# Encoder kernel: first projection units as native FP32 products, a branch split one stage earlier, side units split at the front of their stage

## What is computed

```python
h = rmsnorm(x, norm_g[l])
proj = jnp.einsum('bsd,de->bse', h, w_in[l])          # 42 units, 16 columns ba, 24 gate units
o_a = windowed_gqa(...);  y_a = einsum(o_a * silu(a_z), w_bo_a[l])
o_b = diff_attention(...); y_b = einsum(o_b * silu(b_z), w_bo_b[l])
o_c = rmsnorm(o_fwd + o_bwd, c_norm_g[l])             # two gated delta rules
y_c = einsum(o_c * silu(c_z), w_bo_c[l])
merged = gates[0] * y_a + gates[1] * y_b + gates[2] * y_c
x = x + einsum(merged, w_out[l])
# after both layers: rmsnorm(x, final_g)
```

## Time and profile before

| | us |
|---|---|
| median of 3 runs | 2986.66 |
| lowest, highest | 2984.34, 2987.62 |
| profiled execution, its own time | 2982.72 |
| span in the trace of that execution | 2980.8 |
| PE busy in the span | 2722.8 |
| POOL busy in the span | 1375.6 |
| granted TensorE clock, mean | 0.965 of 2.4 GHz |

### The profile page before, as it was taken

How to read it: one execution, slowest core, us unless ns; L and a number is a source line. 1 busy time by engine, 2 the same in 40 slices (tenths; PEclk the granted TensorE clock), 3 DMA queues, 4 the chain that set the end, 5 groups by cost and what they waited for, 6 DMA issues and landing times. The chain is left out here.

```text
span 2980.8 us, 40155 instructions
## 1 busy us (share of the span) xinstructions
PE 2722.8 (91%) x15402; PEld 2219.3 (74%) x15402; DVE 1593.7 (53%) x1859; ACT 1130.2 (38%) x1866; POOL 1375.6 (46%) x1226
## 2 busy tenths in 40 slices
PE   6989998999889899899879999899998899998995
PEld 4868786777768788777667787777776777896784
DVE  5137646776467443375241565377754864234743
ACT  3024434666345314331111344266653543244111
POOL 4355335343478740265354543444434886304551
PEclk8999999999989999999989999999999999999997
DMA  5253224221344556654242531333213554567431
GB/s 185 71 156 99 79 71 136 85 93 64 124 156 159 170 165 161 227 172 125 68 135 86 148 107 64 112 102 99 86 58 120 193 171 159 164 165 258 129 112 72
DMA packets 394918, 380.51 MB, mean 128 GB/s; under 512 B 91104, under 2 KB 333408, under 8 KB 394720
## 3 DMA queue, kind: packets, MB, share of 16 engines
q1 hardware_dynamic: 355744, 295.87, 33.1%
q10 hardware_dynamic: 38976, 82.00, 7.4%
HBM read 247.70 MB, written 130.09 MB: 127 GB/s over the span
## 5 line engine op out<-in xcount | busy, mean ns | idle before, releaser
L266 PE MATMUL pair<-h_hi,w_hi 128*128 128x512 f32 x1792 | 741.9, 414 | 117.3 <-ACT ev L281 44.8
L246 POOL TENSOR_TENSOR w_hi<-w_stage,masks 128x256 fp32r<-128x256 f32 x432 | 403.6, 965 | 727.3 <-PE pair L266 655.8
L266 PE MATMUL pair<-h_lo,w_hi 128*128 128x512 f32 x1792 | 710.7, 397 | 0.0
L266 PE MATMUL pair<-h_hi,w_lo 128*128 128x512 f32 x1792 | 709.9, 396 | 0.0
L266 PEld LDWEIGHTS pair<-h_hi,w_hi 128*128 128x128 f32 x1792 | 344.1, 192 | 241.7 <-issue 100.8
L266 PEld LDWEIGHTS pair<-h_hi,w_lo 128*128 128x128 f32 x1792 | 343.6, 192 | 75.7
L266 PEld LDWEIGHTS pair<-h_lo,w_hi 128*128 128x128 f32 x1792 | 344.7, 192 | 70.7 <-issue 5.1
L251 POOL TENSOR_TENSOR w_lo<-w_stage,w_hi 128x256 fp32r<-128x256 f32 x432 | 354.5, 852 | 8.5
L281 ACT ACTIVATE ev<-pair 128x512 f32<-128x512 f32 x224 | 132.6, 593 | 492.0 <-PE pair L266 491.8
L217 PE MATMUL pair<-h_hi,w_hi 128*128 128x512 f32 x576 | 183.1, 399 | 41.7 <-DVE h_lo L593 23.9
L2291 POOL TENSOR_TENSOR w_hi<-w_stage,masks 128x512 fp32r<-128x512 f32 (+1 forms) x60 | 103.6, 1727 | 221.0 <-PE pair L217 191.0
(11 more groups left out here) (283 smaller groups left out, 4940.1 us busy)
## 6 DMA issues: line engine op xcount, KB each, us to landing
w_stage<-in_w_in SPq DMA_DIRECT2D x132, 512.0 KB, 4.1
proj<-ev ACTq DMA_DIRECT2D x132, 512.0 KB, 2.7
gate<-proj SPq DMA_DIRECT2D x48, 512.0 KB, 3.6
prep_x<-proj SPq DMA_DIRECT2D x24, 512.0 KB, 4.0
resid<-xT SPq DMA_DIRECT2D x16, 512.0 KB, 8.1
diff_vx<-proj SPq DMA_DIRECT2D x16, 512.0 KB, 3.2
prep_g<-gc_rows SPq DMA_DIRECT2D x16, 512.0 KB, 5.2
qd_t<-prep_eg SPq DMA_DIRECT2D x16, 512.0 KB, 2.6
```

The lines of the kernel that those rows point to most:

```text
L246: last = nc.gpsimd.tensor_tensor(w_hi[s][:, part], w_stage[s][:, part], bcast(ones, PIECE), ALU.mult)
L266: last = nc.tensor.matmul(bank(self.banks[half]), a[s][:, c, :], b[:, c, w], start=(c == 0 and n == 0), stop=(c == KC - 1 and n == 2))
```

## The change

Four things are changed together.

1. **proj.** The load of g and of the weights of units 0 and 1 moves to the end of the stage before (`load_first`, in load and in merge). Units 0 and 1 are no longer split: POOL multiplies their weights by g (`w_g`), PE multiplies them with the unnormalized `xT` in native FP32, and DVE multiplies the results by rstd. The sum of squares comes after chunk 0 of both units. The normalization runs in 16 half chunks through PSUM (`hf` in banks 4 and 5, `rstd_near` in pairs[3]); DVE makes all of `h_lo`. The ba product waits for all of it. POOL sets the next stage's semaphores later, within the stage.
2. **Side units.** win, diff and delta get the scheme of prep. The last split in diff was already absent; those of win (`split(17)`) and prep (`split(17)`) go, and `split(1)` stands at the front of POOL's list in win and diff, and after the memsets in delta. POOL's loop in proj keeps its range up to i = 5 for both slots.
3. **Branch 0** is loaded, rounded and subtracted at the end of delta, into the place of h_hi and h_lo, no longer at the start of merge.
4. **merge.** Heads 0, (1, 2), 3 are gated after steps 4, 5, 6 instead of 0, 1, 2, 3 after 4, 5, 6, 7. For i = OUT the second four chunks of the weights are split before the wait for the slot's last sum.

```diff
-        AHEAD["win"] = SIDE_AHEAD
+        AHEAD["win"] = SIDE_AHEAD_IN
-        AHEAD["diff"] = SIDE_AHEAD
+        AHEAD["diff"] = SIDE_AHEAD_IN
-        AHEAD["delta"] = SIDE_AHEAD
+        AHEAD["delta"] = SIDE_AHEAD_IN
-        AHEAD["merge"] = {"w_lo0": 1, "w_lo1": 1}
+        AHEAD["merge"] = {"w_lo0": 1, "w_lo1": 1, "o_hi": 4, "o_lo": 4}
...
+        def load_first(sp, q, layer, free):
+            sp.wait_ge(q["next_set"], START + 1)
...
+            for s in range(2):
+                free(s)
+                sp.dma_start(w_stage[s][:], w_l[:, :, s * P:(s + 1) * P]).then_inc(after[f"w_in{s}"], 16)
...
# project, POOL
+                    pool.wait_ge(q["g_in"], START + 16)
+                    for c in range(0, KC, PIECE):
+                        part = slice(c, c + PIECE)
+                        for s in range(2):
...
+                            nc.gpsimd.tensor_tensor(w_g[s][:, part], w_stage[s][:, part], cols(g[:, part], P), ALU.mult)\
+                                .then_inc(q["w_scaled"], 1)
...
+                    split(1, 0, first=True)
+                    split(1, 1, first=True)
+                    set_signals("win")
+                    with pool.Fori(2, pairs_of_units + 1) as i:
                         for s in range(2):
                             split(i, s)
# project, PE
-                    units(0)
+                    for k in range(KC):
+                        for s in range(2):
+                            pe.wait_ge(q["w_scaled"], START + k // PIECE * 2 + s + 1)
+                            for half in range(2):
+                                last = nc.tensor.matmul(pairs[s][:, half, :], w_g[s][:, k, :],
+                                                        xT[:, k, half * HALF:(half + 1) * HALF],
+                                                        start=k == 0, stop=k == KC - 1)
...
+                        if k == 0:
+                            total_squares(pe).then_inc(q["total"], 1)
                     pe.wait_ge(q["ba_lo"], START + 1)
+                    pe.wait_ge(q["lo"], START + 2 * KC)
# project, DVE
+                    for j in range(2 * KC):
+                        k, w = j // 2, slice(j % 2 * HALF, (j % 2 + 1) * HALF)
+                        if j >= 2:
+                            dve.wait_ge(q["lo"], START + j - 1)
+                        nc.vector.scalar_tensor_tensor(out=hf[j % 2], in0=xT[:, k, w], scalar=g[:, k:k + 1],
+                                                       in1=rstd_near[:, j % 2, :], op0=ALU.mult, op1=ALU.mult)\
+                            .then_inc(q["scaled"], 1)
+                        if j:
+                            low(j - 1)
+                    low(2 * KC - 1)
...
+                        nc.vector.tensor_tensor(ev[s][:], pairs[s][:].rearrange("p a b -> p (a b)"), rstd[:], ALU.mult)\
+                            .then_inc(q[f"out{s}"], 1)
# win, POOL (diff: only the first line; prep: split(17) removed)
+                    split(1)
...
-                    for k in range(7, UNITS + 2):
+                    for k in range(7, UNITS + 1):
# delta, SP, before the loads of w_bo_a
+                    sp.wait_ge(q["side_sum"], START + 2 * (N_GATE - PREPARED))
+                    for k in range(4):
+                        sp.dma_start(first[:, k, :], gated[k]).then_inc(q["branch_in"], 16)
# delta, POOL
-                    for k in range(2, N_GATE - PREPARED):
+                    for k in range(1, N_GATE - PREPARED):
# delta, ACT, in the last chunk ahead of its copies
+                        else:
+                            act.wait_ge(q["branch_in"], START + 64)
+                            for k in range(4):
+                                nc.scalar.activation(first_hi[:, k, :], first[:, k, :], ACT.Copy).then_inc(q["branch_hi"], 1)
# delta, DVE, at its end
+                    for k in range(4):
+                        dve.wait_ge(q["branch_hi"], START + k + 1)
+                        nc.vector.tensor_tensor(first_lo[:, k, :], first[:, k, :], first_hi[:, k, :].bitcast(F32), ALU.subtract)
# merge, SP
-                    load_branch(0)
...
+                    load_first(sp, q, ds((DEPTH - 1) - l, 1), lambda s: sp.wait_ge(q[f"w_lo{s}"], START + LAST))
# merge, POOL
+                            if i == OUT:
+                                far_stage, far_hi, far_lo = (w[s][:, 4:KC, :] for w in (w_stage, w_hi, w_lo))
+                                nc.gpsimd.tensor_tensor(far_hi, far_stage, bcast(ones, 4), ALU.mult).then_inc(q["far_hi"], 1)
+                                pool.wait_ge(q["far_hi"], START + s + 1)
+                                nc.gpsimd.tensor_tensor(far_lo, far_stage, far_hi.bitcast(F32), ALU.subtract)
                             pool.wait_ge(q[f"sum{s}"], START + i)
# merge, ACT
-                    for s in range(2):
-                        act.wait_ge(q[f"sum{s}"], START + 4)
# merge, DVE
-                            dve.wait_ge(q["normed"], START + h + 1)
-                            nc.vector.tensor_tensor(branch[0][:, h, :], OD[:, h, :], ZT[:, h, :], ALU.mult)\
-                                .then_inc(q["gated"], 1)
-                            low(2, h)
+                            heads = ((0,), (1, 2), (3,), ())[h]
+                            for n in heads:
...
+                            for n in heads:
+                                low(2, n)
```

More of the change, by code:

```diff
@@ L383, in _ @@
                         .then_inc(q["g_in"], 16)
+                    for n in ("g_in", "w_in0", "w_in1"):
+                        sp.wait_ge(signal["proj"][n], START + 16)
                     for t in range(NT):
@@ L436, in project @@
             w_l = w_in.rearrange("l (k p) e -> l p k e", p=P)[ds(l, 1)].rearrange("o p k e -> (o p) k e")
-            with Phase("proj") as (block, q):
+            with Phase("proj", preset=False) as (block, q):
                 top[0] = after_x
-                hf = [sb(f"norm_h{n}", [P, S]) for n in range(4)]
-                rstd = sb("norm_rstd", [P, S])
-                g = small[:, 0:KC]
+                hf = [bank(4), bank(5)]
+                rstd, rstd_near = sb("norm_rstd", [P, S]), pairs[3]
+                w_g = [sb(f"norm_w{s}", [P, KC, P]) for s in range(2)]
+                g = g_next
                 ba_w = sb("ba_w", [P, KC, N_BA])
@@ L568, in outs @@
                                 .then_inc(q[f"put{s}"], 16)
-                    outs(0)
+                    for s in range(2):
+                        act.wait_ge(q[f"out{s}"], START + 1)
+                        act.dma_start(proj[s], ev[s][:]).then_inc(q[f"put{s}"], 16)
                     with act.Fori(1, 2) as i:
@@ L1834, in _ @@
                         products(3, d)
+        delta_o, first_hi, delta_rest, first_lo = (h_start + i * 4 * S * 4 for i in range(4))
+        first_hi = nc.alloc_sbuf_tensor_at("first_hi", [P, 4, S], F32R, offset=first_hi)
+        first = nc.alloc_sbuf_tensor_at("first", [P, 4, S], F32, offset=first_lo)
+        first_lo = nc.alloc_sbuf_tensor_at("first_lo", [P, 4, S], F32R, offset=first_lo)
         def delta_rule(l):
@@ L2321, in high @@
                     def high(br, k):
-                        nc.scalar.activation(o_hi[br % 2][:, k, :], branch[br % 2][:, k, :], ACT.Copy).then_inc(q["o_hi"], 1)
-                    for k in range(4):
-                        act.wait_ge(q[f"in0{k}"], START + 16)
-                        high(0, k)
+                        nc.scalar.activation(branch_hi[br][:, k, :], branch[br % 2][:, k, :], ACT.Copy).then_inc(q["o_hi"], 1)
                     for h in range(4):
```

134 lines of the change are left out of this document (75 added, 59 removed).

## The result

| | us |
|---|---|
| before, median of 4 runs (lowest, highest) | 2987.06 (2984.34, 2987.62) |
| after, median of 4 runs (lowest, highest) | 2943.63 (2938.61, 2949.60) |
| ratio, 95% interval | 0.9858 (0.9845 to 0.9871) |
| span of the profiled execution, before and after | 2980.8, 2943.0 |
| granted clock, mean, before and after | 0.965, 0.971 |

A forecast was written before the change was run, and what follows sets the result against it. PE, busy 91% of the span, was taken as the bound, so only its idle or slow times could gain. Terms summed to 23.1 us per layer, 46 for two, giving 2940, range 2930 to 2957 (0.68).

The forecast's parts named there:

- proj, 14.6 per layer: In proj, native products fill PE's wait beside the norm chain; ba starts at 55.6 instead of 70.20, gaining 14.6 us.
- Branch 0, 6.0 - 0.5 - 1.1: Merge starts 6.0 us sooner per layer, less 0.5 for a colder start and 1.1 for delayed `delta_vw` copies in delta.
- The rival of a late branch: End of delta: branch 0 loads take twice 7.7 us, the loss is 6.8 instead of 1.1, time 2952; chance 0.07.
- Borders of diff and delta, 2.2 each: PE's wait at the start of diff and of delta falls from 6.20 to 3.97 us, gaining 2.2 each per layer.
- The front of diff, 1.9: Split at diff's front delays the sines and `k_lo`, so PE waits for the scores: loss of 1.9 us per layer.
- The front of delta, 0.9: Split after delta's memsets ends at 1057.3, PE wants side unit 1 at about 1056.5: loss of 0.9 us per layer.
- win, 0: No gain at win's start, since POOL's loop in proj still splits unit 11, and no loss from its front split.
- Step 8, 3.0 - 0.5: Merge: gating head 3 after step 6 removes the 2.98 us wait, gain 3.0, less 0.5 for added DVE work, per layer.
- Step 12, 0: Merge: the early split gains 0, since POOL waits for weights to land; PE's wait of 2.69 us stays.
- the serial chain: Rival in proj: scaling, ACT and subtraction run one after another, gain 1.7 instead of 14.6 us, time 2966; chance 0.06.
- the cold clock: Rival in proj: native products stay at half clock, loss of 12.5 us per layer, time 2995; chance 0.03.
- the early parts do more: Rival: merge's step 12 starts 2.7 us earlier and the gap before ba closes, 2 x 3.5, time 2933; chance 0.08.

The follow-up runs named there:

- experiment 5: Changed kernel with the whole projection stage of the kernel before, no `load_first`, all other parts kept: 2975.81 us, ratio 0.9961 to the kernel before.
- experiment 6: Changed kernel with the norm's scaled half chunks and near copy of rstd in SBUF instead of PSUM: 2966.48 us, ratio 0.9934 to the kernel before.
- experiment 4: Changed kernel with branch 0 loaded, rounded and subtracted at the start of merge again: 2954.35 us, ratio 0.9895 to the kernel before.
- experiment 3: Changed kernel with side units of win, diff and delta prepared two ahead again, no front splits: 2944.62 us, ratio 0.9863 to the kernel before.
- experiment 8: Changed kernel without merge's early split, diff two units ahead, unit 11 not split in proj: 2934.40 us; with w_out's early split loaded after step 6: 2930.52 us.
- experiment 2: Changed kernel with heads gated one after each of steps 4 to 7 again: 2949.65 us, ratio 0.9881 to the kernel before.

## Why the prediction was right, point by point

The mechanism of the largest term, the native products beside a norm chain that POOL doesn't slow, was right and carries the result. Two smaller terms were wrong, and that 2943.63 lies within 4 us of 2940 is partly luck.

- **proj, 14.6 per layer**: 16.5 and 15.1, confirmed by experiment 5 (30.0 for two layers). Each step held in layer 0: the start of PE (21.76 for a predicted 22.3), the end of the native records (53.7 for 53.3), the ba product (54.36 for 55.6). The cold start lasted 6 us in place of 4; the norm chain, 22.2 in place of 23.1, gave part of that back, and PE waited 0.68 for it where 2 to 3 were forecast. That the chain isn't slowed with its operands in PSUM was the step on which all hung, and experiment 6 shows its price, 10 us per layer, the amount of two thirds of the gain.
- **Branch 0, 6.0 - 0.5 - 1.1**: 5.9 and 0.9 by experiment 4. PE's wait at the border fell by 6.2 (9.95 to 3.76). The 0.5 for a colder start wasn't there: half clock at the start of merge lasted 3.5 us in layer 0 before and 3.4 after. The copies `delta_vw` wait behind the roundings as said (PE's 1.22, which was 0.49). The rival of a late branch fell: ACT starts the four roundings right behind its own work, at 1205.99.
- **Borders of diff and delta, 2.2 each**: measured on PE, 6.20 to 3.99 and 3.96.
- **The front of diff, 1.9**: mis-sized. The stage grew by 2.1 and 1.1 though its border shrank by 2.2, but layer 0 holds 1.7 of half clock (0.91 at 40 to 60 us) that the kernel before had in layer 1 alone. At the same clock the stage grew by 0.4 and 1.1, so the front costs 2.6 to 3.3. I followed the delayed sine to the scores, where PE doesn't wait; I hadn't followed what is queued behind `diff_q_hi` on ACT. The half collision with DVE is there too: the split's low part takes 3.67 in place of 2.77, DVE's cosine 1.60. With two units ahead diff is about 0.8 us per layer shorter at the same clock (experiment 3).
- **The front of delta, 0.9**: PE's wait before side unit 1 is none in layer 0 and 1.13 in layer 1; the scheme wins 1.2 there (experiment 3).
- **win, 0**: right, and for the reason given; experiment 8 shows it for the border (5.41 to 4.40 without the second split).
- **Step 8, 3.0 - 0.5**: 2.98 became 0.75 and 0.84. Undone alone it is worth 1.9 per layer by the medians (experiment 2), within their scatter; the waits of 3.08 are what shows it.
- **Step 12, 0**: wrong, and the largest miss. I saw rightly that POOL waits for the landing and not for PE, and took "the same data are still to be split" for "the same time". Four instructions of half the size last 8.0 us where two took 6.5 (in layer 1, 7.7 and 5.7), since each can lose time to DVE. That adds to PE's wait, 1.4 in layer 0 and 2.5 in layer 1, and in layer 1 it brings half clock where there was none, for 1.6 more: 5.4 us in all, 2.7 per layer, that should have been in the sum as a loss.

These two misses, 4 us in diff (1.7 of it clock) and 5.5 in merge for the two layers, less 2.4 that proj gives beyond its forecast, are 7 of the 8 us by which the traces differ less than forecast (37.8 for 46); delta has the last one. The medians differ by 43, with the same terms and another draw of the scatter: the time came out nearer than the sum, and that is luck. The rivals of the serial chain, the late branch and the cold clock are excluded by the rows above; that the early parts do more came out the other way.

Open: why TensorE's clock falls behind some waits in one execution and not in another. It sets prep's 242 or 247 us and diff's 343.2 or 344.9, which are the largest part of the scatter that the traces show, in the kernel before (prep 245.4, 242.9) as in all others, and no run here was aimed at it.

## What to carry to other kernels

Moving work ahead of a wait helps only if its input is there by then: ask what has landed, not what is free; and work cut in two beside a busy VectorE can lose time to it twice as often. When an instruction is delayed, look at everything queued behind it on its consumer's engine, not only at the last consumer. And if POOL works beside a chain of DVE, place one operand of each DVE instruction in PSUM: here that alone is worth 10 us per layer. Before a difference of 2 us between two traces is put down to an edit, compare the granted clock of the same stretch in both.

## What the runs showed of the hardware

- A DVE instruction of 512 columns with all operands in SBUF took 2.7 to 2.8 us beside POOL's instructions of 1024 columns, and 0.68 to 0.76 without them or with an input in PSUM. POOL itself lost little (2.48 to 2.79 where it had 2.36).
- At step 12 of merge PE's clock was at half for 3 to 6 us behind waits of 2.68 to 4.06 us (17 cases), sometimes only from the second to the fourth pair on, and at full behind 1.47 to 1.60 (5 cases). At step 8 it stayed at full behind 2.98 and 3.08 (4 cases). Half clock cost 1.6 us where it was measured to the end of the stage (88.9 for 87.3).
- In merge, a POOL instruction that met a DVE instruction of 1024 columns on two SBUF tiles took 0.9 us more at either size: 1.27 to 2.24 at 512 columns, 2.38 to 3.22 at 1024.
- Prep of one layer took 242.3 to 243.8 us at a mean granted clock of 0.96 and 244.9 to 247.2 at 0.94 or 0.95.
